# The last stage of an encoder kernel: the late experts' sums go into the residual on VectorE, and two of four tiles are normalised on ScalarE and GpSimd

## What is computed

```python
def _layernorm(x, g, b):
    mu = jnp.mean(x, -1, keepdims=True)
    var = jnp.mean(jnp.square(x - mu), -1, keepdims=True)
    return (x - mu) * lax.rsqrt(var + LN_EPS) * g + b
...
        y = _grouped_moe(x, router_w, router_bias, moe_w_gate[i], moe_w_up[i], moe_w_down[i])
        x = _layernorm(DEEPNORM_ALPHA * x + y, ln2_g[i], ln2_b[i])
    return x
```

## Time and profile before

| | us |
|---|---|
| median of three runs | 1432.31 |
| lowest and highest run | 1432.04, 1433.28 |
| the profiled execution, whole | 1431.44 |
| its span, first to last instruction | 1429.2 |

### The profile page before, as it was taken

How to read it: one execution, slowest core, us unless ns; L and a number is a source line. 1 busy time by engine, 2 the same in 40 slices (tenths; PEclk the granted TensorE clock), 3 DMA queues, 4 the chain that set the end, 5 groups by cost and what they waited for, 6 DMA issues and landing times. The chain is left out here.

```text
span 1429.2 us, 20767 instructions
## 1 busy us (share of the span) xinstructions
PE 1361.6 (95%) x7302; PEld 801.2 (56%) x7302; DVE 780.6 (55%) x1593; ACT 366.5 (26%) x797; POOL 286.5 (20%) x529
## 2 busy tenths in 40 slices
PE   8889999999999999999998899989899999899996
PEld 5458576685776857768584433336454544633332
DVE  2856766656666566665556443255435454834227
ACT  3322313223132232332221221203323232222210
POOL 2243316033160340603201200030000000200011
PEclk9989999999999999999998999999999999899998
DMA  6440412405124051240713699970111119199983
GB/s 208 123 106 14 110 51 81 137 13 165 50 68 149 13 165 50 57 154 14 243 63 145 258 413 413 389 264 1 62 38 40 42 40 347 79 357 413 412 323 115
DMA packets 173330, 220.89 MB, mean 155 GB/s; under 512 B 57360, under 2 KB 107920, under 8 KB 173264
## 3 DMA queue, kind: packets, MB, share of 16 engines
q1 hardware_dynamic: 141744, 173.66, 34.9%
q10 hardware_dynamic: 26432, 28.32, 5.8%
q0 software_dynamic: 5088, 18.02, 3.5%
HBM read 185.63 MB, written 34.34 MB: 154 GB/s over the span
## 5 line engine op out<-in xcount | busy, mean ns | idle before, releaser
L509 PE MATMUL bank<-xT,wgu 128*128 128x512 f32 x448 | 196.5, 597 | 3.3 <-DVE wgu L1183 3.3
L1967 PE MATMUL bank<-wgu,moe_xgT 128*32 128x512 f32 x1536 | 169.8, 594 | 1.2 <-issue 0.9
L509 PEld LDWEIGHTS bank<-xT,wgu 128*128 128x128 f32 x448 | 84.5, 191 | 105.2 <-issue 105.2
L557 PE MATMUL bank<-wd,oT 128*128 128x512 f32 x256 | 123.6, 623 | 2.8 <-ACT oT L916 1.6
L591 PE MATMUL bank<-wd,xT 128*128 128x256 f32 x512 | 119.7, 379 | 0.0
L1183 DVE SCALAR_TENSOR_TENSOR wgu<-bank,taps,wgu 128x510 f32<-128x510 f32 (+1 forms) x128 | 95.3, 745 | 41.7 <-ACT wgu L794 36.7
L1967 PEld LDWEIGHTS bank<-wgu,moe_xgT 128*32 128x32 f32 x1536 | 49.1, 110 | 103.6 <-issue 91.8
L591 PEld LDWEIGHTS bank<-wd,xT 128*128 128x128 f32 x512 | 95.3, 190 | 14.4 <-issue 2.9
L1990 PE MATMUL bank<-wd,moe_hidT 128*32 128x512 f32 x768 | 87.0, 593 | 4.1 <-DVE moe_hidT L2238 3.1
L2234 DVE TENSOR_TENSOR moe_hid<-moe_silu,bank 128x256 f32<-128x256 f32 x24 | 10.1, 422 | 126.5 <-ACT moe_silu L2077 126.5
L557 PEld LDWEIGHTS bank<-wd,oT 128*128 128x128 f32 x256 | 47.5, 198 | 52.2 <-issue 49.1
(11 more groups left out here) (352 smaller groups left out, 2319.6 us busy)
## 6 DMA issues: line engine op xcount, KB each, us to landing
wgu<-moe_w_gate SPq DMA_DIRECT2D x32, 1024.0 KB, 13.4
wgu<-moe_w_up SPq DMA_DIRECT2D x32, 1024.0 KB, 14.9
wd<-moe_w_down SPq DMA_DIRECT2D x32, 1024.0 KB, 15.0
wgu<-dn_w_in SPq DMA_DIRECT2D x32, 512.0 KB, 5.2
slots_x<-gains SPq DMA_DIRECT2D x5, 1920.0 KB, 10.9
wd<-dn_w_in SPq DMA_DIRECT2D x8, 1024.0 KB, 6.6
wd<-dn_w_out ACTq DMA_DIRECT2D x16, 512.0 KB, 4.0
xT<-slots_x ACTq DMA_DIRECT2D x16, 512.0 KB, 8.2
```

The source lines that it names most:

```text
L509: mm = pe.matmul(bank[:], wqkv[:, ct, k], xT[:, k], start=k == 0, stop=k == KD - 1)
L557: mm = pe.matmul(ps[uses.at[f"{name}{n}"][0]][:], oT[:, h, tt], wo[:, h, half * 512:(half + 1) * 512], start=h == 0, stop=h == 1)
L1967: mm = pe.matmul(ps[2][seats].rearrange("p (a f) -> p a f", a=2), xgT[:, j % ROW_BUFS, k, seats], wgu[:, e % RING, :, k], start=k == 0, st ...
```

## The change

TensorE no longer multiplies the residual by the identity. It computes the late products alone, and VectorE adds each bank to `res` (`meet`). The statistics and the normalisation then read `res` in SBUF. Tiles 1 and 3 are normalised on VectorE (`gain_sums`). For tiles 0 and 2, GpSimd computes -mean * rstd (`shift_sums`), ScalarE applies rows * rstd + shift in two halves (`scale_sums`), and GpSimd multiplies by the gain and adds the bias over 1024 columns each (`weigh_rows`). VectorE's queue becomes meet(0), spread(0), add(1), meet(1), spread(1), add(2), meet(2), spread(2), gain(1), add(3), meet(3), spread(3), gain(3). GpSimd's becomes fetch, root(0), shift(0), root(1), weigh(0), root(2), shift(2), root(3), weigh(2). The last tile is stored in two halves, one from ScalarE's queue and one from SyncE's.

```diff
-    def combine_all(self, pe, tt):
-        for half in range(2):
-            bank, cols = self.t["ps"][2 * tt + half], slice(half * 512, (half + 1) * 512)
-            for q in range(LATE):
-                pe.matmul(bank[:], late_gates(self.t, q)[:, tt * P:(tt + 1) * P], late_rows(self.t, q)[:, cols], start=q == 0, stop=False)
-            if tt:
-                pe.wait_ge(self.added, 2 * tt)
-            pe.matmul(bank[:], self.t["const"][:, C_ID:C_ID + P], self.t["res"][:, tt, cols], start=False, stop=True).then_inc(self.combined, 1)
...
+    on_vector, on_scalar_rows = (1, 3), (0, 2)
...
+    def gain_sums(self, dve, tt):
+        rows, n = self.t["res"][:, tt], self.on_vector.index(tt)
+        dve.wait_ge(self.t["gain_in"][self.which], 32)
+        dve.wait_ge(self.centred, tt + 1)
         for half in range(2):
             cols = slice(half * 512, (half + 1) * 512)
-            ins = self.nc.vector.scalar_tensor_tensor(out=rows[:, cols], in0=self.t["ps"][2 * tt + half][:], scalar=self.neg[:, tt:tt + 1], in1=self.g[:, cols], op0=ALU.add, op1=ALU.mult)
-        ins.then_inc(self.centred, 1)
-        dve.wait_ge(self.centred, 2 * tt + 2 + ahead)
+            ins = self.nc.vector.scalar_tensor_tensor(out=rows[:, cols], in0=rows[:, cols], scalar=self.neg[:, tt:tt + 1], in1=self.g[:, cols], op0=ALU.add, op1=ALU.mult)
+        ins.then_inc(self.gained, 1)
+        dve.wait_ge(self.gained, n + 1)
         dve.wait_ge(self.rstd_ready, tt + 1)
-        self.nc.vector.scalar_tensor_tensor(out=rows, in0=rows, scalar=self.rstd[:, tt:tt + 1], in1=self.b, op0=ALU.mult, op1=ALU.add).then_inc(self.normed, 1)
+        for half in range(2):
+            cols = slice(half * 512, (half + 1) * 512)
+            self.nc.vector.scalar_tensor_tensor(out=rows[:, cols], in0=rows[:, cols], scalar=self.rstd[:, tt:tt + 1], in1=self.b[:, cols], op0=ALU.mult, op1=ALU.add).then_inc(self.normed, 1)
+
+    def shift_sums(self, pool, tt):
+
+        pool.wait_ge(self.centred, tt + 1)
+        pool.wait_ge(self.rstd_ready, tt + 1)
+        self.nc.gpsimd.tensor_tensor(self.shift[:, tt:tt + 1], self.neg[:, tt:tt + 1], self.rstd[:, tt:tt + 1], ALU.mult).then_inc(self.shifted, 1)
+
+    def scale_sums(self, act, tt):
+
+        act.wait_ge(self.shifted, self.on_scalar_rows.index(tt) + 1)
+        for half in range(2):
+            part = self.t["res"][:, tt, half * 512:(half + 1) * 512]
+            act.activation(part, part, ACT.Identity, bias=self.shift[:, tt:tt + 1], scale=self.rstd[:, tt:tt + 1]).then_inc(self.scaled, 1)
+
+    def weigh_rows(self, pool, tt):
+
+        rows, n = self.t["res"][:, tt], self.on_scalar_rows.index(tt)
+        pool.wait_ge(self.t["gain_in"][self.which], 32)
+        pool.wait_ge(self.scaled, 2 * n + 2)
+        self.nc.gpsimd.tensor_tensor(rows, rows, self.g, ALU.mult).then_inc(self.weighted, 1)
+        pool.wait_ge(self.weighted, n + 1)
+        self.nc.gpsimd.tensor_tensor(rows, rows, self.b, ALU.add).then_inc(self.rows_done, 1)
...
-            for tt in range(TT):
-                sp.wait_ge(rows.normed, tt + 1)
+            for tt in (0, 1, 2):
+                if tt in rows.on_vector:
+                    sp.wait_ge(rows.normed, 2 * rows.on_vector.index(tt) + 2)
+                else:
+                    sp.wait_ge(rows.rows_done, rows.on_scalar_rows.index(tt) + 1)
                 sp.dma_start(out[0, tt * P:(tt + 1) * P], t["res"][:, tt]).then_inc(stored, 16)
-            sp.wait_ge(stored, 16 * TT)
+            sp.wait_ge(rows.normed, 4)
+            sp.dma_start(out[0, 3 * P:, 512:], t["res"][:, 3, 512:]).then_inc(stored, 16)
+            sp.wait_ge(stored, 16 * (TT + 1))
+
+        @block.scalar
+        def _(act):
+            for tt in rows.on_scalar_rows:
+                rows.scale_sums(act, tt)
+            act.wait_ge(rows.normed, 3)
+            act.dma_start(out[0, 3 * P:, 0:512], t["res"][:, 3, 0:512]).then_inc(stored, 16)
...
             for tt in range(TT):
-                back.combine_all(pe, tt)
+                back.combine(pe, tt)
...
             for tt in range(TT):
                 rows.root(pool, tt)
+                if tt in rows.on_scalar_rows:
+                    rows.shift_sums(pool, tt)
+                if tt % 2:
+                    rows.weigh_rows(pool, tt - 1)
...
-            back.add(dve, 1)
-            back.add(dve, 2)
-            for tt in range(TT):
+            back.meet(dve, 0)
+            rows.spread(dve, 0)
+            for tt in range(1, TT):
+                back.add(dve, tt)
+                back.meet(dve, tt)
+                rows.spread(dve, tt)
                 if tt == 2:
-                    back.add(dve, 3)
-                rows.spread_sums(dve, tt, back)
-                if tt:
-                    rows.apply_sums(dve, tt - 1)
-            rows.apply_sums(dve, TT - 1)
+                    rows.gain_sums(dve, 1)
+            rows.gain_sums(dve, 3)
```

More of the change, by code:

```diff
@@ L1663 @@
 class LastRows(Arrival):
[L1666 to L1679, removed]
+    on_vector, on_scalar_rows = (1, 3), (0, 2)
+    def __init__(self, nc, t, sb, sem, which):
+        super().__init__(nc, t, sb, sem, which)
+        self.shift = sb("shift", [P, TT])
+        self.gained, self.shifted, self.scaled, self.weighted, self.rows_done = (sem(n) for n in ("gained", "shifted", "scaled", "weighted", "rows_done"))
```

## The result

The changed kernel took 1433.78 us in the median of 22 runs, the kernel before 1430.87 in as many: a ratio of 1.0031 with a 95% interval of 1.0019 to 1.0042, or +4.4 us (+2.7 to +6.0). The ratio agrees with that of the mean times (1434.7 and 1430.2, 4.5 us apart); the two medians are only 2.9 us apart. The kernel is slower, by somewhat less than the prediction gave: its +6.2 lies just outside the interval.

The account below looks back on a forecast made before the run. The prediction took VectorE's queue after the last barrier, held up by GpSimd's passes, as the bound: it ends +6.6 us later, +6.2 with the store tail. Added to the 1432.3 us median this gave 1438.5 us, range 1436.5 to 1440.

Parts of the forecast that it names:

- The head of the queue: VectorE's start of the last stage: meet(0) waits for TensorE's banks, done 4.40 us in, 3.1 us of it waiting.
- Unit costs: VectorE's price per operation: spread 1.77 us, add 2.63, meet 1.31 with its wait, gain step 2.60, half pass 0.68.
- VectorE's sum: VectorE's load in the last stage without collisions: 25.9 us before, 25.5 after, so it hardly moves.
- ScalarE's two halves: ScalarE's scaling of tiles 0 and 2: some 1.25 us in halves, hidden behind GpSimd's root(1) or root(3).
- The GpSimd passes: GpSimd's weigh_rows: each 128x1024 pass takes 2.36 us, bounds 2.2 to 2.54.
- The long turns: VectorE's gain(1) and gain(3) stand behind GpSimd's long passes; gain(1) waits 1.4 us for weigh(0)'s bias sum.
- The short turns: GpSimd's powers and shift(2) hold VectorE: 0.25 us each at add(1) and add(2), then +0.1, +0.3, +0.1 at gain(1).
- The tail: After VectorE's end: last 256 KB store lands in 2.1 to 2.7 us, then 1.2 to the end of the span.
- The first: Rival for VectorE and GpSimd's last stage: no collision costs anything, GpSimd ends last, +2.7 us, 1435.0; chance 0.12.
- The second: Rival at VectorE's spreads and meets: GpSimd holds these too, a further 1.5 to 2.5 us, 1440 to 1441; chance 0.1.
- The third: Rival of a faster kernel: GpSimd passes under 1.3 us, half-sized last store gives 0.6 back, 1431.7 or below; chance 0.02.
- The fourth: Rival of partial collisions, for example GpSimd's long passes waiting for VectorE: +2.9 to +4.5 us, 1435.2 to 1436.8; chance 0.14.

Follow-up runs that it names:

- e1_no_weigh: The changed kernel without GpSimd's two long gain and bias passes for tiles 0 and 2: VectorE ended at 28.7 us, last stage 32.0 us.
- e2_gains_in_psum: The changed kernel with gain and bias rows copied by TensorE into free PSUM banks for VectorE's gain steps: VectorE ended at 28.9 us, stage 36.4 us.
- e4: The changed kernel with GpSimd's weigh_rows of tile 2 placed ahead of root(3): VectorE ended at 32.1 us, stage 35.9 us.
- h1_one_tile_off: Kernel before the change, add(3) ahead of spread(1), only tile 0 handed to ScalarE and GpSimd in half passes: ratio 0.9975, stage 29.9 us.

## Why the prediction was right, step by step

**The head of the queue.** VectorE was past meet(0) 4.44 us after the first product (1395.88 - 1391.44), 4.40 predicted. **Unit costs.** Adds, meets and statistics were as taken. Two small ones were off in opposite directions: a half gain pass with both inputs in SBUF is 0.75 and not 0.68 (1.41 for two in e1_no_weigh), and the two gain steps of that run took 2.78 and 2.87 and not 2.60, 0.45 together; three of the four spreads took 1.63 or 1.64 and not 1.77 (the first from 1395.88 to 1397.51), 0.4 together. That VectorE's sum hardly moves was shown by e1_no_weigh (28.7 against 28.6). ScalarE's two halves took 1.52 and not 1.25, and hid behind GpSimd's roots as expected.

**The GpSimd passes.** 2.34 alone, 2.36 predicted. **The long turns.** Predicted 1.4 at gain(1), and 2.0 and 2.1 at the two bias halves (its ends 1426.4, 1429.1 and 1431.9, less 0.68 for each pass); measured 2.17 - 0.75 = 1.42, 2.71 - 0.75 = 1.96 and 2.82 - 0.75 = 2.07. These are the terms that carry the result, and they held to 0.1 us.

**The short turns were a wrong term.** The prediction let the powers and shift(2) hold VectorE as long passes do: 0.25 twice, 0.5 at gain(1), 0.4 at gain(3). With operations of one column the engines exclude each other in one direction only. In the fence, of the kernel after, the power ends at 1399.22, 0.4 into VectorE's second pass, which keeps its 1.28:

```profile
1397.51 1.27 DVE L1650 SCALAR_TENSOR_TENSOR res<-wgu,gate,res 128x1024 f32<-128x1024 f32 x1
1397.76 1.46 POOL L173 TENSOR_TENSOR last_row_rstd<-last_row_rstd,masks 128x1 f32<-128x1 f32 x1
1398.82 1.28 DVE L1650 SCALAR_TENSOR_TENSOR res<-wd,gate,res 128x1024 f32<-128x1024 f32 x1
```

The four terms are 1.4 us together, and none of them was there. With the 0.2 by which the unit costs were short, VectorE was +5.5 late and not +6.6. The step that failed reads rows 9: they show that the power stands behind VectorE, and the converse was assumed from rows 8, which are of long passes.

**The tail** went the other way. From VectorE's end to the end of the span it took 1430.1 - 1425.57 = 4.5, where the prediction had 3.3 to 3.9: it priced the last half at 2.1 to 2.7, and it landed in 2.8 behind tile 2; and it took the 1.2 from landing to end over from the kernel before, where 1.7 was measured. So VectorE's end was forecast 1.1 too late and the tail up to 1.2 too short. That these two errors cancel, and the stage is +6.1 against +6.2, is luck; what the prediction had right is the long turns. The whole time came out at +4.4. The 6.1 lie just above the end of its interval (+6.0), and with runs of one kernel 9 to 10 us apart what took the difference is not shown; nothing in the code ahead of the stage changed.

**The rivals.** The first (no collision costs anything) put the end on GpSimd; e2_gains_in_psum made that case, GpSimd ended last at 31.4, and it is not what happens with both inputs in SBUF. The second (spreads and meets held too) fell with the rows of after and of e4. The third needed GpSimd passes under 1.3 us; they are 2.34. The fourth, partial collisions of +2.9 to +4.5, can't be told from the forecast by the whole time, since +4.4 would fit it too. It falls by the stage, which is +6.1, and by the trace: GpSimd's two long passes take turns with VectorE's bias halves, and VectorE ends last, at 34.1 against GpSimd's 33.6.

## What to carry to other kernels

Work that is moved from VectorE to GpSimd is only off the path where VectorE meanwhile runs instructions with at most one input in SBUF: place it under those, or move one of VectorE's operands to PSUM. Count the turns before counting the relief: here 5.4 us were moved and 5.5 us were lost again. And before relieving an engine, see whether its time shows as a hole that a reordering fills: moving one add in the queue made VectorE end 1.1 us earlier (h0_add_earlier), where the change made it end 5.5 later.

## What the runs showed of the hardware

A GpSimd pass of 128x1024 on two SBUF inputs takes 2.34 us, and a VectorE pass with two SBUF inputs that asks meanwhile ends 0.5 to 0.6 (half pass) or 1.1 (whole pass) after it; the reverse ends 2.2 after. In the collisions read here the pass that asked first went first, even by 0.1 us (h1_one_tile_off). The power of one column on GpSimd stands behind VectorE (0.54 becomes 0.92 to 1.46) but does not hold it. That differs from the page "SBUF — State Buffer" of the Trainium skill (section "SBUF: two separate sides"), which has the engine that starts first keep the shared ports for its whole instruction; the 1.28 beside the power is the measurement, and it decides. In which part of its time the power needs the ports is not shown. A 256 KB store at the end lands in 2.0 to 2.1 us when no other was issued shortly ahead of it, and in 2.7 to 2.9 when a 512 KB store was issued within 0.6 us ahead of it (after twice, e2_gains_in_psum). From the last landing to the end of the span it is 1.2 to 1.3 us, or 1.7 in the kernels where GpSimd applies gain and bias.
